# A two-layer encoder step on one core: where the sparse mixer splits and turns its keys

## The reference

```python
def indexer_scores(qi, wi, ki):
    s = jnp.einsum('bqhd,bsd->bqhs', qi, ki).astype(jnp.float32)
    return jnp.einsum('bqhs,bqh->bqs', jax.nn.relu(s), wi.astype(jnp.float32)) * (IDX_DIM ** -0.5 * IDX_HEADS ** -0.5)
...
        sc = indexer_scores(qiblk, wblk, ki)
        sc = jnp.where((key_chunk[None, :] <= q_chunk[:, None])[None], sc, -jnp.inf)
        _, idx = lax.top_k(sc, k_sel)
        valid = (idx // CHUNK) <= q_chunk[None, :, None]
        return selected_attention(qblk, gather_rows(k, idx), gather_rows(v, idx), valid)
```

## Time and profile before

| | us |
|---|---|
| median of 3 runs (2753.3 to 2759.3) | 2757.02 |
| the profiled execution | 2753.92 |
| its span, first to last instruction | 2752.2 |

### The profile page before, as it was taken

The page is one execution under the profiler, slowest core; times in us unless marked ns, Lnnn a source line. Parts: engine busy times, 40 slices in busy tenths (PEclk is TensorE's granted clock), DMA queues, the critical chain, the costliest instruction groups (busy, mean ns, idle before and its releaser), DMA issues. The chain is left out here.

```text
span 2752.2 us, 36437 instructions
## 1 busy us (share of the span) xinstructions
PE 2613.0 (95%) x14198; PEld 2298.3 (84%) x14198; DVE 1449.1 (53%) x2754; ACT 992.7 (36%) x1890; POOL 182.9 (7%) x168
## 2 busy tenths in 40 slices
PE   7999999999999999979878998889999999999996
PEld 6777779999989898877667888877898989999895
DVE  2435364444454444566676789864635444444435
ACT  3206334222323232322766655562532323222231
POOL 0300030000000000110030000001300000000003
PEclk9999999999999999989986999899999999999998
DMA  4110311101101010121200000012110101010111
GB/s 134 50 33 10 113 37 62 62 31 39 53 30 61 30 61 31 55 86 42 64 8 1 1 1 1 8 55 94 62 41 31 61 30 61 30 61 30 34 43 65
DMA packets 81279, 124.25 MB, mean 45 GB/s; under 512 B 6224, under 2 KB 54736, under 8 KB 81168
## 3 DMA queue, kind: packets, MB, share of 16 engines
q1 hardware_dynamic: 81168, 122.74, 13.5%
HBM read 110.98 MB, written 11.75 MB: 45 GB/s over the span
## 5 line engine op out<-in xcount | busy, mean ns | idle before, releaser
L1219 PE MATMUL psum<-xt_hi,layer_w_hi 128*128 128x384 f32 (+1 forms) x1536 | 505.5, 329 | 3.2 <-DVE xt_lo L853 3.2
L1221 PE MATMUL psum<-xt_hi,layer_w_lo 128*128 128x384 f32 (+1 forms) x1536 | 505.1, 329 | 0.0
L1220 PE MATMUL psum<-xt_lo,layer_w_hi 128*128 128x384 f32 (+1 forms) x1536 | 504.9, 329 | 0.0
L1134 DVE TENSOR_TENSOR act<-psum,act 128x512 f32<-128x512 f32 x540 | 366.3, 689 | 233.5 <-PE psum L1257 230.7
L1255 PE MATMUL psum<-layer_w_hi,layer_h_split 128*128 128x512 f32 x1024 | 400.0, 391 | 2.8 <-DVE layer_h_split L1122 1.6
L1256 PE MATMUL psum<-layer_w_lo,layer_h_split 128*128 128x512 f32 x1024 | 399.3, 390 | 0.0
L1257 PE MATMUL psum<-layer_w_hi,layer_h_split 128*128 128x512 f32 x1024 | 399.1, 390 | 0.0
L1219 PEld LDWEIGHTS psum<-xt_hi,layer_w_hi 128*128 128x128 f32 x1536 | 288.3, 188 | 4.7 <-DVE xt_lo L853 3.5
L1220 PEld LDWEIGHTS psum<-xt_lo,layer_w_hi 128*128 128x128 f32 x1536 | 288.4, 188 | 1.3
L1221 PEld LDWEIGHTS psum<-xt_hi,layer_w_lo 128*128 128x128 f32 x1536 | 288.4, 188 | 0.0
L1122 DVE TENSOR_TENSOR layer_h_split<-layer_h_raw,layer_h_split 128x384 fp32r<-128x384 f32 (+1 forms) x192 | 98.4, 512 | 352.8 <-ACT layer_h_split L1035 352.8
(11 more groups left out here) (240 smaller groups left out, 4245.4 us busy)
## 6 DMA issues: line engine op xcount, KB each, us to landing
layer_w_raw<-in_ff_w SPq DMA_DIRECT2D x64, 1024.0 KB, 6.4
ab_in_w_raw<-in_ab_w_in SPq DMA_DIRECT2D x12, 512.0 KB, 3.9
c_in_w_raw<-in_c_w_in SPq DMA_DIRECT2D x12, 512.0 KB, 3.8
ab_in_xt_raw<-in_xT SPq DMA_DIRECT2D x8, 512.0 KB, 4.1
layer_resid<-in_x SPq DMA_DIRECT2D x16, 256.0 KB, 2.7
x_scratch<-act SPq DMA_DIRECT2D x8, 512.0 KB, 2.6
layer_resid<-x_scratch SPq DMA_DIRECT2D x16, 256.0 KB, 2.7
out_y_prompt<-act SPq DMA_DIRECT2D x8, 512.0 KB, 2.6
```

The costliest lines, as they stand in the source:

```text
L1134: dve.tensor_tensor(acc, banks[4 + g % 4][0:r], acc, ALU.add).then_inc(y_read, 1)
L1219: pe.matmul(out, w1_hi[:, k, w], xt_hi[:, k, a:b], start=(k == 0), stop=False)
L1220: pe.matmul(out, w1_hi[:, k, w], xt_lo[:, k, a:b], start=False, stop=False)
L1221: mm = pe.matmul(out, w1_lo[:, k, w], xt_hi[:, k, a:b], start=False, stop=(k == KT - 1))
```

## The change

- The prologue keeps key slot 0 alone. The other keys go as units between the heads: `unit_at` puts units 1 to 12 behind heads 2, 4, 6, 15, 18, 21, 24, 31, 33, 35, 37 and 40. Unit 1 is key slot 1, units 2 and 3 the index keys (slots 0 to 5 only, since later index products need no more), units 4 to 6 the sample's three slots, units 7 to 12 slots 2 to 7.
- A unit passes through the two transposing banks: a group of high parts, which ScalarE copies, and a group of low parts, which VectorE copies one head later (`unit_low`). ScalarE's cast for the next unit stands behind the copy, GpSimd's subtraction beside it.
- The 14 steps of `cuts.mask` go two to a head behind the scores of heads 1 to 7 (CUT_AT). `settle` stays ahead of head 0, behind the copy of slot 0's low part.
- The index products of ranked tile 3 move from heads 2, 3, 6, 7 to heads 10, 11, 14, 15, their mixes to heads 12, 13, 15, 16. Its rounds go 13, 11, 8 over heads 18 to 47, 48 to 63, 64 to 79, where they went 14, 10, 8 over heads 9 to 47, 48 to 63, 64 to 79.
- In `block_c_in` slot 26 has no bisection steps; the later ones move one slot back, to slot 33 for one tile and slot 34 for the other.

The diff, cut to its core (`unit` stands twice: first ScalarE's, last TensorE's; `unit_low` is VectorE's):

```diff
         steps_at = {}
-        for i, (slot, a_slot) in enumerate([(2 * NT - 1, 2), (2 * NT, 2)]):
+        for i, first in enumerate([2 * NT - 1, 2 * NT]):
+            slots = [g for g in range(first, 4 * NT) if g != 3 * NT - 1]
             for k in range(STEPS):
-                steps_at.setdefault(slot + k // a_slot, []).append((k % a_slot, i, k))
+                steps_at.setdefault(slots[k // 2], []).append((k % 2, i, k))
...
-    begin = {m: 4 if m == SCORED_EARLY else HP * (m - 1) for m in range(SCORED_EARLY, NR)}
+    begin = {m: 12 if m == SCORED_EARLY else HP * (m - 1) for m in range(SCORED_EARLY, NR)}
...
-    for m, parts in {3: [(14, 9, 48), (10, 48, 64), (8, 64, 80)], 4: [(5, 53, 64), (12, 64, 80), (15, 80, 96)],
+    for m, parts in {3: [(13, 18, 48), (11, 48, 64), (8, 64, 80)], 4: [(5, 53, 64), (12, 64, 80), (15, 80, 96)],
...
+    IDX_SLOTS = max(blocks(t) for t in RANKED[SCORED_EARLY:])
+    UNITS = [("k", [0]), ("k", [1]), ("idx", [0, 1, 2, 3]), ("idx", list(range(4, IDX_SLOTS)))]
+    UNITS += [("k", [sl]) for sl in (NP_TILES, NP_TILES + 1, OWN, 2, 3, 4, 5, 6, 7)]
+    unit_at = {x: 1 + n for n, x in enumerate([2, 4, 6, 15, 18, 21, 24, 31, 33, 35, 37, 40])}
+    CUT_AT = 1
...
+            def unit(u):
+                    copy(k_hh[:, :, k0:k0 + r], quads(bank, r))
...
             k_high(0)
             q_high(0)
+            k_high(1)
+            unit(0)
             for g in range(4):
                 queries(0, g)
...
+                    if x in unit_at:
+                        unit(unit_at[x])
+                        if unit_at[x] + 1 < len(UNITS):
+                            k_high(unit_at[x] + 1)
...
+            def unit_low(u):
+                dve.wait_ge(turned, low_group[u] + 1)
+                if kind == "k":
+                    dve.tensor_copy(k_ll[:, :, k0:k0 + r], quads(bank, r)).then_inc(low_copied, 1)
...
+            unit_low(0)
             cuts.settle(dve, counts)
-            for i in range(len(BISECTED)):
-                cuts.mask(dve, i, counts[:, 0], counts[:, 1])
...
+                if x - 1 in unit_at:
+                    unit_low(unit_at[x - 1])
+                for step in range(2 * (x - CUT_AT), 2 * (x - CUT_AT) + 2):
+                    if 0 <= step < len(BISECTED) * cuts.MASK_STEPS:
+                        cuts.mask(dve, step // cuts.MASK_STEPS, step % cuts.MASK_STEPS, counts[:, 0], counts[:, 1])
...
+            def unit(u):
+                for split, made in ((kh, kh_made), (kl, kl_made)):
+                    pe.wait_ge(made, u + 1)
+                    group([(b * P, split[u % KRING][0:r, b * P:(b + 1) * P], r)
+                           for b in range(C_KV if kind == "k" else len(slots))], ident_r)
```

More of the change, by code:

```diff
@@ L2118, in group, with wait_copied @@
                 n[0] += 1
-            flat = lambda x: x.rearrange("p two d -> p (two d)")
-            turn = lambda bank, at, src: pe.transpose(bank[:, at:at + src.shape[0]].bitcast(F32R), src,
-                                                      ident_r[0:src.shape[0], 0:src.shape[0]])
+            by_vector = sorted(low_group.values())
+            def wait_copied(groups):
+                before = sum(g < groups for g in by_vector)
+                if before and by_vector[before - 1] == groups - 1:
+                    pe.wait_ge(low_copied, before)
+                else:
+                    pe.wait_ge(copied, groups - before)
+            flat = lambda x: x.rearrange("p two d -> p (two d)")
+            def unit(u):
+                kind, slots = UNITS[u]
+                r = srows(slots[0])
+                for split, made in ((kh, kh_made), (kl, kl_made)):
+                    pe.wait_ge(made, u + 1)
+                    group([(b * P, split[u % KRING][0:r, b * P:(b + 1) * P], r)
+                           for b in range(C_KV if kind == "k" else len(slots))], ident_r)
             def queries(p, g):
@@ L2159, in scores @@
                 if h == 0:
-                    pe.wait_ge(copied, query_groups[p])
+                    its_keys = [u for u, (kind, slots) in enumerate(UNITS)
+                                if kind == "k" and slot0(t) <= slots[0] < slot0(t) + blocks(t)]
+                    wait_copied(query_groups[p])
+                    pe.wait_ge(low_copied, max(its_keys) + 1)
                 out = banks_of(("head", x))
```

159 lines of the change are left out of this document (80 added, 79 removed).

## The result

The changed kernel takes 2773.9 us (median of 10 runs, 2767.8 to 2782.0), the kernel before 2756.1 beside it (10 runs, 2748.3 to 2759.3). The ratio is 1.007, with an interval of 1.0056 to 1.0084: slower by 18 us, where 7 us less were forecast.

The account below looks back on a forecast made before the run. VectorE was taken to bound tiles 0 and 1, TensorE the sample tile. Terms -27.3 + 8.0 + 2.1 + 5.0 + 4.5 + 0.5 = -7.2 us took 2757.0 to 2749.8 us; range 2739 to 2763.

Parts of the forecast that it names:

- head 0's scores: End of the prologue: VectorE's scores of head 0 at 1427.0, between 1425.1 and 1428.4, where they stood at 1454.3.
- heads 0 to 7: Tile 0's first half: VectorE sets the pace, 22.3 us for what took 14.3; 8.0 lost (5.6 to 11.0).
- heads 8 to 15: Tile 0's second half: four index products and tile 1's queries, 16.5 us against 14.4; 2.1 lost (0 to 4).
- tile 1: Heads 16 to 31: 25.0 us against 20.0, from halves at the low and full clock; 5.0 lost (3.8 to 8).
- sample tile: From head 32: TensorE is the bound, four units add 1.1 us each; 4.5 lost (2.2 to 7).
- head 48 against before: End of the sample tile: head 48's scores near 1523, where they stood at 1530.4.
- Prologue: Ahead of head 0: with only slot 0's chain left, head 0 comes 27.3 us earlier (25.9 to 29.2).
- a sign of being wrong: Ahead of the mixer: the prediction is wrong if the input block ends later than 1416.9.
- Masks: Heads 1 to 7 on VectorE: the two masks take 17.5 us (15.1 to 20.5), the scan under 3 us.
- Low copies: On VectorE: three add 1.8 us in heads 0 to 7, four 2.5 in tile 1, five 3.4 in the sample tile.
- Rival 1: Clock stays at 0.50 through tile 1 to the sample tile's end: +13.4 us, 2770.4 us; chance 0.08.
- Rival 2: Units between heads: TensorE stalls on GpSimd's low parts, 1.25 us each, 11 us for nine: +4, 2761 us; chance 0.15.

Follow-up runs that it names:

- e12: Changed kernel with ScalarE instead of VectorE copying the units' low parts, a repeat of e5: 2749.0 us, ratio 0.9982 to the kernel before.
- e1: Kernel before with only the bisection's new slots (slot 26 empty, last steps in slots 33 and 34): 2751.7 us, ratio 0.9994.
- e9: e5 plus a VectorE pass of the copy's size, on an unused tile, wherever a low copy of units 1 to 12 stood: 2747.9 us, ratio 0.997.
- e5: Changed kernel with the units' low parts copied by ScalarE behind the high ones, so VectorE waits for no unit: 2746.2 us, ratio 0.996.

## Why the prediction was wrong, step by step

Its steps against the trace of the changed kernel and of e12, which is the same but for who copies:

| | before | forecast | changed | e12 |
|---|---|---|---|---|
| head 0's scores | 1454.3 | 1427.0 | 1427.7 | 1428.3 |
| heads 0 to 7, us | 14.3 | 22.3 | 26.7 | 21.0 |
| heads 8 to 15 | 14.4 | 16.5 | 18.3 | 15.4 |
| tile 1 | 20.0 | 25.0 | 32.6 | 23.4 |
| sample tile | 27.4 | 31.9 | 47.2 | 34.4 |
| head 48 against before | | -7.7 | +22.0 | -7.9 |

- **Prologue** (-27.3 forecast, -26.5 measured): right in size, in part by luck. The mixer began 2.3 us late, which the prediction had named as a sign of being wrong and which e1 and e12 show to vary from run to run, and its prologue took 8.6 us where 10.1 were forecast. The forecast let VectorE's `settle` of up to 8.1 us set head 0; it took 3.8 and ended at 1426.3, and the first scores waited for TensorE, 8.6 us after the start, near the 8.2 that the prediction had as its lower end. TensorE's waits for GpSimd's low keys are one of 1.0 us.
- **Masks** (17.5 us): right. The steps as they ran in heads 1 to 7 sum to 18.2, and the scan is under 3 us, as said:

```profile
L1516 DVE TENSOR_TENSOR_SCAN c_mix_cut_counts<-c_mix_cut_counts 128x1024 f32<-128x1024 f32 x1 | 2.3, 2291 | 0.0
L1516 DVE TENSOR_TENSOR_SCAN c_mix_cut_counts<-c_mix_cut_counts 128x896 f32<-128x896 f32 x1 | 2.0, 2019 | 0.0
```

- **Low copies**: this is the step that failed. "Three low copies add 1.8", "four low copies 2.5" and "five copies 3.4" price only their busy time. That was right (0.69 each), and e9 shows that busy time costs nothing. But each is also a new wait on VectorE, with the next head's maximum, the masks' steps and the rounds queued behind it, and the sum had no term for that. The prediction asked who TensorE waits for at a unit, and never whom VectorE waits for. In heads 0 to 7 the three waits (1.58, 1.58 and 1.32 us) sum to 4.5, and the stretch is 4.4 us over its forecast; at full clock those of tile 1 cost 4.1, and in the sample tile they cost 13.0 through the clock.
- **Tile 1 and the sample tile without these waits**: the sample's units were priced too low, 31.9 us against 34.4 in e12. For tile 1 the prediction's own halves, 14.8 and 11.9, sum to 26.7, and it took 25.0 without saying why; e12 has 23.4, e5 24.6.
- **Rival 1** (low clock through tile 1 and the sample, 2770.4 us, chance 0.08) is near what happened: tile 1 was priced at 29.6 and took 32.6; the sample's heads were to grow by 16 and are 15.3 over the forecast. The size was right, the chance and the way there weren't. The low clock didn't outlive tile 1: it ended at 1495.7, was full for 17 us, and fell anew at 1512.6. And the rival tied the low clock to VectorE as the bound of tiles 0 and 1. e12 has the same bound, fuller than the changed kernel, and is at full clock in tile 1. What stands ahead of the second fall is a short idle gap of TensorE in a tile where each engine waits for the next, and the copies made such gaps. The argument against, "at 1.2 GHz TensorE needs 1.57 of every 1.57 us in tile 1, so it is full, and the clock came back there", doesn't carry over to the sample tile: full at 1.2 GHz from 1513 on, TensorE didn't get the clock back for 44 us.
- **Rival 2** (units stall on GpSimd, 2761): not seen. Between the heads no wait of TensorE for GpSimd is in the trace.
- **The gain itself**: the forecast of -7.2 lies between what e5 and e12 measure, -11 and -5. So without the change of copier the kernel is about where the prediction put it, in part by luck: in e12 heads 0 to 7, heads 8 to 15 and tile 1 came out 1.1 to 1.6 us under their forecasts, the sample tile 2.5 over. The range, 2739 to 2763, ended below rival 1's own time.

What stays open: why all sets together cost 24 us, when alone the sample's cost 12 and the other two nothing; and what a gap does to the clock. The gap of 0.75 us in the changed kernel was followed by 44 us at 1.2 GHz. One of 0.74 in e12 (to 1516.8) was followed by 6 (1520 to 1526), and one of 0.75 in e9 by none, both ahead of an index product late in the sample tile:

```profile
1523.00:1524.00 1.00, 0.25 (x2) 0.17 (x2) 0.88 (x3) 0.78 (x3) 0.00 (x0) 1.00 0.00 0
1524.00:1530.00 6.00, 6.00 (x43) 4.41 (x43) 2.14 (x5) 3.22 (x11) 0.00 (x0) 1.00 0.00 0
```

## What to carry to other kernels

A copy that is handed to a less busy engine brings its wait along. Price that wait, and what is queued behind it, apart from the copy's busy time: the engine with time to spare can be the one that must not stand, since it feeds all others. Where three engines hand each other work within a head, put the copy on the engine that already waits for that producer in that place (here ScalarE, whose next copy waits for the same transposes), or far enough behind that the producer is surely done. And where a change puts small stalls of TensorE into a stretch at full clock, keep a rival with the whole stretch at 1.2 GHz, priced from rows at that clock.
